# A Strassen-type feed-forward kernel on one core: weight sums built in place in two PSUM banks, and the seven products in another order

## The reference

```python
def half_swiglu(x, g, w_up, w_down):
    h = rms_norm(x, g)
    a, b = jnp.split(h @ w_up, 2, axis=-1)
    return x + 0.5 * ((jax.nn.silu(a) * b) @ w_down)
# per layer: x = half_swiglu(...); x = x + mix(...); x = half_swiglu(...)
```

## Time and profile before

| | |
|---|---|
| median of 3 runs | 2734.58 us (2734.44 to 2734.65) |
| profiled execution, its span | 2732.7 us; the measured time has about 1.9 us more around a span |
| PE busy | 2707.3 us (99%) |
| DVE busy | 1729.2 us (63%) |
| ACT busy | 1103.5 us (40%) |
| POOL busy | 999.8 us (37%) |
| mean granted PE clock | 9 in every one of the 40 slices (full speed) |

### The profile page before, as it was taken

One profiled execution on the slowest core, in us unless ns is written; L12 is line 12 of the kernel. 1 busy time (PEld: TensorE's weight loads), 2 busy tenths in 40 slices (PEclk: granted clock), 3 DMA queues, 4 the chain that ended last, 5 costly groups with the idle time before them and its releaser, 6 DMA issues. The chain is left out here.

```text
span 2732.7 us, 46951 instructions
## 1 busy us (share of the span) xinstructions
PE 2707.3 (99%) x18804; PEld 2646.4 (97%) x18804; DVE 1729.2 (63%) x2801; ACT 1103.5 (40%) x1858; POOL 999.8 (37%) x610
## 2 busy tenths in 40 slices
PE   9999999999999999999999999999999999999998
PEld 8999999998999999999999999999989999999997
DVE  8747576887433693838685647668773347837475
ACT  5324244636322352424443333454463224424242
POOL 2333333345433333333333333333544333333332
PEclk9999999999999999999999999999999999999999
DMA  3222222233122222222222222222332222222222
GB/s 118 99 71 93 77 87 93 88 124 125 63 71 91 75 73 84 78 93 78 94 77 85 70 95 78 92 86 88 132 109 70 77 88 74 75 79 78 93 78 85
DMA packets 72853, 238.04 MB, mean 87 GB/s; under 512 B 8304, under 2 KB 17264, under 8 KB 72176
## 3 DMA queue, kind: packets, MB, share of 16 engines
q1 hardware_dynamic: 57888, 208.30, 22.1%
q10 hardware_dynamic: 14800, 27.51, 2.9%
HBM read 227.52 MB, written 8.27 MB: 86 GB/s over the span
## 5 line engine op out<-in xcount | busy, mean ns | idle before, releaser
L498 POOL TENSOR_TENSOR w_lo<-w_raw,w_hi 128x1024 fp32r<-128x1024 f32 (+1 forms) x254 | 600.0, 2365 | 962.8 <-ACT w_hi L1131 947.7
L1131 ACT ACTIVATE w_hi<-w_raw 128x1024 fp32r<-128x1024 f32 (+1 forms) x238 | 250.2, 1051 | 796.1 <-PE lin L635 660.8
L635 PE MATMUL lin<-h_hi,w_hi 128*128 128x320 f32 x1600 | 373.8, 315 | 2.9 <-DVE tmp L1614 2.7
L635 PE MATMUL lin<-h_hi,w_lo 128*128 128x320 f32 x1600 | 364.6, 309 | 0.0
L635 PE MATMUL lin<-h_lo,w_hi 128*128 128x320 f32 x1600 | 364.1, 309 | 0.0
L635 PE MATMUL lin<-g_hi,w_lo 128*128 128x320 f32 x1408 | 320.9, 309 | 0.0
L635 PE MATMUL lin<-g_lo,w_hi 128*128 128x320 f32 x1408 | 320.8, 309 | 0.0
L635 PE MATMUL lin<-g_hi,w_hi 128*128 128x320 f32 x1408 | 320.7, 309 | 0.0
L550 POOL TENSOR_TENSOR lo_A<-raw_even,hi_A 128x512 fp32r<-128x512 f32 x120 | 167.8, 1398 | 376.3 <-ACT hi_A L1185 376.3
L635 PEld LDWEIGHTS lin<-h_hi,w_hi 128*128 128x128 f32 x1600 | 265.2, 188 | 15.9 <-issue 11.3
L635 PEld LDWEIGHTS lin<-h_lo,w_hi 128*128 128x128 f32 x1600 | 267.5, 188 | 0.0
(11 more groups left out here) (334 smaller groups left out, 6215.6 us busy)
## 6 DMA issues: line engine op xcount, KB each, us to landing
w_raw<-wts SPq DMA_DIRECT2D x240, 512.0 KB, 3.5
raw_even<-wts SPq DMA_DIRECT2D x88, 512.0 KB, 4.4
raw_odd<-wts SPq DMA_DIRECT2D x64, 512.0 KB, 4.2
caches<-kcache_in ACTq DMA_DIRECT2D x16, 512.0 KB, 4.0
caches<-vcache_in ACTq DMA_DIRECT2D x16, 512.0 KB, 4.7
x<-x_in SPq DMA_DIRECT2D x8, 320.0 KB, 6.6
k_out<-kT ACTq DMA_DIRECT2D x2, 1280.0 KB, 4.6
v_out<-v_sb ACTq DMA_DIRECT2D x2, 1280.0 KB, 8.6
```

The source lines that it names most:

```text
L498: ins = nc.gpsimd.tensor_tensor(w_lo[:, s, cols], w_raw[:, s, cols], w_hi[:, s, cols].bitcast(F), ALU.subtract)
L635: ins = nc.tensor.matmul(out[:, half, :], w, a[:, half * HALF:(half + 1) * HALF], start=first and n == 0, stop=last and n == 2)
L1131: nc.scalar.activation(w_hi[:, s, 0:cols], w_raw[:, s, 0:cols], ACT.Copy).then_inc(hi_ready.sem, 1)
```

## The change

Three things change in the pairs' part of the feed-forward.

First, for every pair but the first of a segment, S1 is written to one of two PSUM banks (`chain`, the two halves of `lin[1]`, which the down projection uses and the products do not), S2 is made in place over it, and S4 in place over S2. S2 therefore can only be made after the lo of S1 has been taken. Pair 0 of a segment keeps its sums in SBUF.

Second, PE's order is M1 M5 M6 M4(i-1) M3(i-1) M2 M7: M5 moves from the end of a pair to its second place.

Third, the hand-written lists of ACT and DVE are put in another order to go with it.

```diff
-        S2_sum = [at("S2_sum0", ...), at("S2_sum1", ...)]
+        S2_sum = at("S2_sum", [P, 4 * P], F, cos_at + strip)
+        chain = [lin[1][:, 0, :], lin[1][:, 1, :]]
...
 # PE, segment(), for i in 1..e
                     if i == 1:
                         pe.wait_ge(evacuated.sem, evacuated.count(L, m))
+                    m5(L, q + i, i)
                     m6(L, q + i, i)
...
                     m2(L, q + i, i)
                     m7(L, q + i, i)
-                    m5(L, q + i, i)
                 m4(L, q + e, e)
...
 # ACT, segment()
                     if more:
                         hi_strip(L, q + i + 1, i + 1, "A11", "M1")
-                        if g or i > 1:
-                            hi_strip(L, q + i + 1, i + 1, "S2", "M6")
-                    hi_strip(L, q + i, i, "A22", "M4" if i else None)
-                    hi_strip(L, q + i, i, "S4", "M3" if i else None)
+                        hi_strip(L, q + i + 1, i + 1, "S1", "M5")
+                    if not i:
+                        hi_strip(L, q, 0, "A22")
+                        hi_strip(L, q, 0, "S4")
+                    if more:
+                        hi_strip(L, q + i + 1, i + 1, "S2", "M6")
                     if i:
+                        hi_strip(L, q + i, i, "A22", "M4")
+                        hi_strip(L, q + i, i, "S4", "M3")
                         silus(L, q + i - 1, i - 1)
...
 # DVE, add_strips()
+                elif name == "S2" and i:
+                    dve.wait_ge(strip_ready["S1"].sem, strip_ready["S1"].count(L, q + 1))
+                    out, a, b, op = link, link, raw_[:, 0, :], ALU.subtract
...
 # DVE, first_pair() (g = 0)
-                add_strips(L, q + 1, 1, "S1")
+                add_strips(L, q + 1, 1, "S1", m)
+                add_strips(L, q + 1, 1, "S3")
+                lo_strip(L, q + 1, 1, "S1")
                 add_strips(L, q + 1, 1, "S2")
-                add_strips(L, q + 1, 1, "S3")
-                lo_strip(L, q + 1, 1, "S2")
                 lo_sums(L, f, "T4")
...
                 keep_u3(L, q, 0)
                 c22(L, q, 0)
                 lo_tokens(L, f, 2)
+                lo_strip(L, q + 1, 1, "S2")
                 add_strips(L, q + 1, 1, "S4")
...
 # DVE, segment()
-                    keep_u3(L, q + i, i)
-                    if more:
-                        lo_strip(L, q + i + 1, i + 1, "S3")
-                    if i:
                         lo_g(L, q + i - 1, slot0 + i - 1)
+                keep_u3(L, q + e, e)
                 c22(L, q + e, e)
```

More of the change, by code:

```diff
@@ L1181, in hi_strip @@
                     act.wait_ge(sums_done[name].sem, sums_done[name].count(L, q + 1))
-                src = raw_pair[i % 2][:, block_[name], :] if name in block_ else (S1_sum if name == "S1" else S2_sum[i % 2])[:, :]
-                if early:
-                    src = S4_sum[:, :]
+                if name in block_:
+                    src = raw_pair[i % 2][:, block_[name], :]
+                elif i:
+                    src = chain[i % 2]
+                else:
+                    src = (S1_sum if name == "S1" else S4_sum if early else S2_sum)[:, :]
                 nc.scalar.activation(strip_hi[name][:, :], src, ACT.Copy).then_inc(strip_hi_done[name].sem, 1)
@@ L1689, in closing, with add_strips @@
                 reciprocal_root(L, p)
-            def add_strips(L, q, i, name):
+            def add_strips(L, q, i, name, m=None):
                 raw_ = raw_pair[i % 2]
+                link = chain[i % 2]
                 if name == "S1":
                     sem, count = pairs_landed(L, q)
-                    if q:
+                    if i >= 2:
+                        dve.wait_ge(strip_ready["S4"].sem, strip_ready["S4"].count(L, q - 1))
+                    elif i:
+                        dve.wait_ge(evacuated.sem, evacuated.count(L, m))
+                    elif q:
                         dve.wait_ge(strip_ready["S1"].sem, strip_ready["S1"].count(L, q))
                     dve.wait_ge(sem, count)
-                    out, a, b, op = S1_sum[:, :], raw_[:, 2, :], raw_[:, 3, :], ALU.add
+                    out, a, b, op = link if i else S1_sum[:, :], raw_[:, 2, :], raw_[:, 3, :], ALU.add
+                elif name == "S2" and i:
+                    dve.wait_ge(strip_ready["S1"].sem, strip_ready["S1"].count(L, q + 1))
+                    out, a, b, op = link, link, raw_[:, 0, :], ALU.subtract
                 elif name == "S2":
@@ L1702, in add_strips @@
                     if q >= 2:
-                        dve.wait_ge(strip_ready["S4"].sem, strip_ready["S4"].count(L, q if i == 0 else q - 1))
-                    out, a, b, op = S2_sum[i % 2][:, :], S1_sum[:, :], raw_[:, 0, :], ALU.subtract
+                        dve.wait_ge(strip_ready["S4"].sem, strip_ready["S4"].count(L, q))
+                    out, a, b, op = S2_sum[:, :], S1_sum[:, :], raw_[:, 0, :], ALU.subtract
                 elif name == "S3":
+                    if i:
+                        dve.wait_ge(sums_done["S1"].sem, sums_done["S1"].count(L, q + 1))
                     out, a, b, op = raw_[:, 2, :], raw_[:, 0, :], raw_[:, 2, :], ALU.subtract
@@ L1708, in add_strips @@
                     dve.wait_ge(strip_ready["S2"].sem, strip_ready["S2"].count(L, q + 1))
-                    out, a, b, op = S2_sum[i % 2][:, :], raw_[:, 1, :], S2_sum[i % 2][:, :], ALU.subtract
+                    kept = link if i else S2_sum[:, :]
+                    out, a, b, op = kept, raw_[:, 1, :], kept, ALU.subtract
                 nc.vector.tensor_tensor(out, a, b, op).then_inc(sums_done[name].sem, 1)
             def lo_strip(L, q, i, name):
-                src = {"S1": S1_sum[:, :], "S2": S2_sum[i % 2][:, :], "S4": S2_sum[i % 2][:, :],
+                kept = chain[i % 2] if i else S2_sum[:, :]
+                src = {"S1": chain[i % 2] if i else S1_sum[:, :], "S2": kept, "S4": kept,
                        "S3": raw_pair[i % 2][:, 2, :], "A11": raw_pair[i % 2][:, 0, :],
@@ L1793, in lo_last, with first_pair @@
                                         ALU.subtract).then_inc(g_ready.sem, 1)
-            def first_pair(L, f, q, n):
+            def first_pair(L, f, q, n, m):
                 lo_strip(L, q, 0, "S2")
@@ L1936, in ffn @@
                 for g in range(len(GROUPS)):
-                    segment(L, f, g, q, n0)
+                    segment(L, f, g, q, n0, m0)
                     q += SEGMENTS[g]
```

49 lines of the change are left out of this document (23 added, 26 removed).

## The result

The changed kernel takes 2804.06 us (median of 4 runs, 2803.71 to 2809.06) against 2734.51 us: ratio 1.0259, 95% interval 1.0245 to 1.0274. It is slower by 2.6%. The forecast was 2785 us with a range from 2759 to 2802: the sign was right, the size 19 us short, and the time lies 2 us outside the range. The profiled execution has a span of 2801.7 us, 69.0 more than before.

The account below looks back on a forecast made before the run. The prediction took PE to bound the kernel, idle only 25.4 us. Stalls of 31.7 at segment ends, 8.5 at beginnings with g = 1 or 2 and 10.8 with g = 0 gave 2785 us, range 2759 to 2802.

Parts of the forecast that it names:

- PE as the bound: Whole kernel: PE busy 2707.3 us of a 2732.7 us span, only 25.4 us idle, its work the same after the change.
- the middle of a segment: Pairs inside a segment: inputs stay in time, with 1.9 us slack before M1(i+1); cost 0.
- the middle stalls too: Rival, pairs inside segments: late weights would cost each of some 60 pairs 0.3 us, + 18, 2804 us; chance 0.14.
- Price of sums in PSUM: DVE's sums: a PSUM operand costs nothing extra, and sums no longer held by POOL free about 1 us per pair.
- The tails: Segment ends, 12 times: M4(e) waits for keep_u3(e), queued behind lo_g(e-1), which POOL holds; 2.64 us each, 31.7 us.
- The heads with g = 1 and 2: Beginnings of 8 segments: M7(0) waits for keep_u2(0), queued behind S1's lo and the S2 sum; 1.06 each, 8.5 us.
- The beginning with g = 0: Four segment beginnings: DVE's queue delays M6(1), M4(1) and M1(3); three times 2.8 plus net 2.5, sum 10.8 us.
- PE's clock falls in the new pauses: Rival, twelve pauses of 2.6 us: each costs one product at half rate, 1.76 us, + 21, 2807 us; chance 0.06.
- the main sum: Whole kernel: the stalls at segment ends and beginnings add 51.0 us to the time before.
- the main case: Whole kernel: the predicted stalls without any rival, 2785.6 us, alone 2776 to 2792; chance 0.61.

Follow-up runs that it names:

- run 9: Changed kernel with keep_u3(e) ahead of lo_g(e-1), M5(e) behind M7(e), keep_u2(0) earlier where g = 1 or 2, and other DVE and ACT orders at g = 0: 2735.17 us.
- run 3: Changed kernel with ACT's hi of the gated block ahead of its split of the down weights at segment ends: 2771.97 us.
- run 1: Changed kernel with keep_u3 of a segment's last pair ahead of lo_g of the pair before it on DVE: 2773.68 us.
- run 4: Kernel before the change with M5(e) moved ahead of M2(e), so that M4(e) follows M7(e): 2745.53 us.
- run 10: Kernel before the change with M5(e) ahead of M2(e) on PE and keep_u3(e) behind lo_g(e-1) on DVE: 2745.68 us.
- run 6: Changed kernel with keep_u3(e) ahead of lo_g(e-1) and, where g = 1 or 2, keep_u2(0) ahead of S1's lo of pair 1: 2765.77 us.
- run 2: Changed kernel with 20 matmuls whose result nobody reads put between M7 and M4 of each segment's last pair, waits unchanged: 2794.59 us.
- run 5: Changed kernel with keep_u2(0) ahead of S1's lo of pair 1 in segments with g = 1 or 2: 2802.68 us.
- run 11: Kernel before the change with M5(e) ahead of M4(e-1) on PE and keep_u3(e) behind lo_g(e-1) on DVE: 2780.95 us.
- run 8: Changed kernel with other orders of DVE's and ACT's lists at the beginning of the four g = 0 segments: 2784.48 us.
- run 7: Changed kernel with M5 of each segment's last pair back behind M7(e), on PE alone: 2769.69 us.

## Why the prediction fell short

**PE as the bound, and the middle of a segment: right.** PE's work stayed the same, no product in the middle waits, and the rival "the middle stalls too" is out: run 9 has the new order in every pair but a segment's last and costs 0.7 us, inside its interval.

**Price of sums in PSUM: right.** No more than 0.03 us extra by the groups after, and nothing in the time by run 9. What stood beside it was wrong: DVE's busy time did not fall by some 60 us, it rose by 6.8. The sums themselves did get cheaper, but POOL's operations met S3 and lo_g instead. The step counted the meetings removed and not the new ones. That this cost nothing in the middle is DVE's slack there, not the step's merit.

**The tails: right.** Forecast 12 x 2.64 = 31.7, measured 12 x 2.60 = 31.2, with the forecast's mechanism: lo_g held by POOL (run 3), in front of keep_u3 (run 1), and a bare minimum of 0.91 (run 4). The working gave both conditions but I read them too narrowly later: run 10 had to teach me that the two products between M3(e-1) and M4(e) are part of it.

**The heads with g = 1 and 2: right.** Forecast 8 x 1.06 = 8.5, measured 8 x 1.04 = 8.3, confirmed by run 6.

**The beginning with g = 0: nearly the right sum from partly wrong steps, which is luck.** Forecast 10.8, measured 12.5. M6(1) waits as forecast for S2's lo (1.25 + 0.10 against 1.47). But "M4(1) is about 0.7 late, and the Silu of pair 1 about 1.0 late for M1(3)" did not happen; M1(2) waits 2.51 + 0.10 us for the Silu of pair 0. I followed lo_g(0) and pair 1's Silu from DVE's queue and overlooked that `lo_last`, and c12(0) behind it, release M1(2) by the Silu of pair 0. In the three later segments that makes 3 x 3.55 instead of 3 x 2.8; the first has a net 1.8 against 2.5.

**The clock: the step that failed.** In the prediction it is the rival "PE's clock falls in the new pauses", 12 falls of 1.76 us, +21, with a chance of 0.06. It came true in part: 11 falls, 17.2 us; the main sum of 51.0 is 52.0 as measured, and 52.0 + 17.2 is what happened. The main sum put this term at 0. The rival's price was right within 5 us, its chance was not. I argued from the pauses in front of products that the trace of before had, up to 1.4 us, which say nothing of pauses twice as long. And "granted in full throughout" was wrong. The waits of PE before, of which the earlier trace rows shows a part, begin with a pause of 3.1 us in front of a matmul that is not in a product, 10.5 us before the program's end, and from 2722.18 on the clock is at 0.50 (the row, then two stretches of before):

```profile
PE bank L757 <- DVE tmp L1655: 3.1, 1, 3.1
...
2720.00:2722.00 2.00, 0.00 (x0) 0.00 (x0) 1.83 (x4) 0.00 (x0) 0.00 (x0) 1.00 0.00 0
2722.00:2724.00 2.00, 0.91 (x8) 0.51 (x8) 0.96 (x3) 0.00 (x0) 0.00 (x0) 0.55 0.00 0
```

The 40 slices of the page are too coarse to show it. PE had little to do around that pause, so it alone didn't prove a fall behind 2.5 us in a busy stretch, but it speaks against a chance as low as 0.06.

The Trainium skill states that an array left idle goes back to half its clock (TensorE: Matmul & The Clock Gate, Part 1). The traces agree, with 0.50 in the stretch at 2446. The fall's price belonged beside each term that makes a pause long, not in a rival by itself, since it applies to whatever case makes those pauses: the main case with the measured falls is 2785.6 + 17.2 = 2802.8. Open is what decides between a fall and none behind two pauses of the same length. Runs 2, 5 and 11 show only that it isn't the place in the program. It seems to differ between executions of one kernel too: of the changed kernel's four, those of 2803.71 to 2804.24 us had a mean granted clock of 0.991, the one of 2809.06 had 0.989.

## What to carry to other kernels

Where a product order is changed, count the products between the one that starts a chain on the other engines and the one that waits for it, and follow every engine's list between them; which product stands next to which says little. Price a stall of a saturated PE together with what its clock does behind it: here 2.5 us cost 4.1 us where the clock fell, and a mended stall of 1 us elsewhere can seem worthless since the falls behind other pauses shift. Time freed on an engine that isn't the bound is worth nothing by itself. Here moving DVE's operands to PSUM moved the meetings with POOL to its other operations rather than ending them.

## What the runs showed of the hardware

The clock fell to half for a few microseconds behind 8 of 12 pauses of 2.5 us at the tails in the changed kernel, 11 of 12 in run 5, 6 of 12 in run 8 and 9 of 12 in run 11, and behind none of the pauses of up to 1.6 us in front of products in any run. The shortest with a fall behind it was 2.2 us (run 1, the first M1(2)). One fall cost 1.3 to 1.6 us; behind the pause of 3.8 us it cost 2.6 in the changed kernel and 2.5 in run 7. Small matmuls in the pause prevented it (run 2). A 128x640 operation of DVE with both operands in SBUF took 0.83 us alone (run 3) and 2.46 us beside POOL (run 10).
